# Sums of weight quarters in the delta-net projection, by accumulating DMAs instead of GpSimd arithmetic

## The reference, cut to what matters

```python
def gated_deltanet(h, w_in, conv_w, a_log, dt_bias, norm_w, w_out):   # h: 512 x 1024
    proj = h @ w_in                      # w_in: 1024 x 4112, float32
    qkv, z, a, bt = jnp.split(proj, ...) # q, k, v, z: 8 heads x 128 columns each
    qkv = silu(causal_dwconv(qkv, conv_w))
...
```

## Time and profile before

| What | Value |
|---|---|
| device time, median of 3 runs | 2596.41 us (2595.0 to 2597.74) |
| span of the profiled execution | 2595.1 us |
| PE busy | 2532.1 us (98% of the span) |
| DVE busy | 1643.4 us (63%) |
| POOL busy | 252.9 us (10%), of it 91.4 us in the four lines of sums |
| bytes moved by DMA | 276.81 MB |
| delta-net with its projection | from 40 us to about 450 us of the span |

### The profile page before, as it was taken

How to read it: one execution, slowest core, us unless ns; L and a number is a source line. 1 busy time by engine, 2 the same in 40 slices (tenths; PEclk the granted TensorE clock), 3 DMA queues, 4 the chain that set the end, 5 groups by cost and what they waited for, 6 DMA issues and landing times.

```text
span 2595.1 us, 32921 instructions
## 1 busy us (share of the span) xinstructions
PE 2532.1 (98%) x13038; PEld 1999.9 (77%) x13038; DVE 1643.4 (63%) x2905; ACT 719.3 (28%) x1381; POOL 252.9 (10%) x186
## 2 busy tenths in 40 slices
PE   6999999999999999999999999999999999999999
PEld 3777775688888888888888888886445568888888
DVE  2787875687776365455648777745375486666652
ACT  3555553321110122211203111004253375222200
POOL 1434331100000030000001000001121000000000
PEclk9999999999999999999999999999999999999999
DMA  8222311243433321122023453331021310212121
GB/s 350 109 79 74 131 74 72 91 185 146 188 142 144 120 77 70 69 83 84 33 97 130 163 195 148 137 122 69 33 83 65 130 66 33 93 70 98 67 90 55
DMA packets 26377, 276.81 MB, mean 107 GB/s; under 512 B 3689, under 2 KB 4585, under 8 KB 9201
## 3 DMA queue, kind: packets, MB, share of 16 engines
q1 hardware_dynamic: 23040, 268.92, 27.1%
q10 hardware_dynamic: 3184, 5.78, 0.7%
HBM read 272.58 MB, written 2.11 MB: 106 GB/s over the span
## 4 chain that ended last, share of the span: by engine, by line
PE 87%; DVE 7%; ACT 3%; DMA 2%; issue 1%; POOL 0%; SPq 0%; ACTq 0%; DVEq 0%; POOLq 0%
PE bank L688 29%; PE bank L772 15%; PE bank L2583 11%; PE bank L1467 5%; PE bank L2996 5%; PE bank L2369 4%; PE bank L419 3%; DVE arena L1906 1%; PE bank L2674 1%; DMA arena<-w_ada 1%; PE bank L501 1%; PE bank L2989 1%; PE bank L1617 1%; PE bank L1605 1%; PE bank L3139 1%
## 5 line engine op out<-in xcount | busy, mean ns | idle before, releaser
L688 PE MATMUL bank<-HT,ring 128*128 128x256 f32 x1056 | 248.0, 380 | 2.0 <-ACT HT L1104 2.0
L688 PE MATMUL bank<-arena,ring 128*128 128x256 f32 x1056 | 249.5, 379 | 0.0
L688 PE MATMUL bank<-arena 128*128 128x256 f32 x1056 | 249.5, 379 | 0.0
L688 PEld LDWEIGHTS bank<-HT,ring 128*128 128x128 f32 x1056 | 199.3, 190 | 34.2 <-issue 5.2
L688 PEld LDWEIGHTS bank<-arena,ring 128*128 128x128 f32 x1056 | 200.6, 190 | 27.3
L688 PEld LDWEIGHTS bank<-arena 128*128 128x128 f32 x1056 | 200.6, 190 | 27.3
L772 PE MATMUL bank<-arena,ring 128*128 128x256 f32 x936 | 207.0, 379 | 1.4 <-ACT arena L845 1.4
L772 PEld LDWEIGHTS bank<-arena,ring 128*128 128x128 f32 x936 | 177.4, 190 | 27.1 <-ACT arena L845 2.6
L1328 ACT ACTIVATE arena<-bank,ffc 128x512 f32<-128x512 f32 x66 | 51.3, 777 | 487.3 <-DVE bank L1234 487.3
L1133 POOL TENSOR_SCALAR XT<-XT,comb_v 128x512 f32<-128x512 f32 x32 | 50.1, 1577 | 1049.3 <-ACT HT L1104 652.3
L2996 PE MATMUL bank<-HT,ring 128*128 128x512 f32 x320 | 146.5, 598 | 0.5 <-ACT HT L1145 0.5
(11 more groups left out here) (509 smaller groups left out, 4403.5 us busy)
## 6 DMA issues: line engine op xcount, KB each, us to landing
ring<-w_ada SPq DMA_DIRECT2D x33, 2048.0 KB, 7.5
ring<-w_up SPq DMA_DIRECT2D x33, 2048.0 KB, 7.4
ring<-w_down SPq DMA_DIRECT2D x24, 1408.0 KB, 6.0
ring<-w_gdn SPq DMA_DIRECT2D x7, 2048.0 KB, 8.9
ring<-w_ret_qk SPq DMA_DIRECT2D x4, 2048.0 KB, 8.2
ring<-w_ret_v SPq DMA_DIRECT2D x4, 2048.0 KB, 8.2
ring<-w_ret_g SPq DMA_DIRECT2D x4, 2048.0 KB, 8.3
ring<-w_ret_out SPq DMA_DIRECT2D x4, 2048.0 KB, 8.3
```

Of the source, the lines that this page charges most:

```text
L688: last = nc.tensor.matmul(out_, w[:, k, :], x[:, k, :], start=(first and k == 0), stop=(k == 3), skip_group_check=not first)
```

## The change

The four sums of a pair become DMAs of 256 KB with `accum_op=add`, issued from POOL's queue. A DMA can only add, so S3 = A11 + A21, S2 = S3 + A22, S1 = A21 + A22 and S4 = A12 + S2 are made, and the signs are turned in the input's sums and where the results are put together. S3, S2 and S1 add a quarter that is read again from the weights in memory; S4 adds S2 from SBUF. For S1 the place of A11 must first hold A21: ACT loads it anew from memory (256 KB, plain) behind `keep_m1`, after a wait for S3's landing. PE waits for the landings in place of POOL's counter. POOL waits for S2's landing before it issues S4, and for ACT's load before S1. Ten semaphores are added.

```diff
+        gdn_sum_in = {name: [sem(f"gdn_{name}_in{p}") for p in range(2)] for name in ("S1", "S2", "S3", "S4", "A21")}
...
-                        pe.wait_ge(pool_done, at("pool", "gdn", "S3", h, p))
+                        pe.wait_ge(gdn_sum_in["S3"][p], 16 * (h + 1))
...
                 nc.scalar.activation(gdn_m1, B[p][:, 0:TH], ACT.Copy).then_inc(act_done, AC.tick("gdn", "m1", h, p))
+                act.wait_ge(gdn_sum_in["S3"][p], 16 * (h + 1))
+                A11, u = gdn_quarters(h, p)[0], GDN_UNITS[p][1]
+                act.dma_start(A11.rearrange("p k n -> p (k n)"), dr["w"]["gdn"][h][:, u * KC * P:u * KC * P + 4 * P]).then_inc(gdn_sum_in["A21"][p], 16)
...
-                nc.vector.tensor_tensor(gdn_t, Bg[:, TH:T], gdn_m7, ALU.add).then_inc(dve_done, DV.tick("gdn", "t", h, p))
+                nc.vector.tensor_tensor(gdn_t, gdn_m7, Bg[:, TH:T], ALU.subtract).then_inc(dve_done, DV.tick("gdn", "t", h, p))
...
-            nc.vector.tensor_tensor(gdn_T[2], HR[:, 4:8, :], HR[:, 0:4, :], ALU.subtract).then_inc(dve_done, DV.tick("gdn", "T3"))
+            nc.vector.tensor_tensor(gdn_T[2], HR[:, 0:4, :], HR[:, 4:8, :], ALU.subtract).then_inc(dve_done, DV.tick("gdn", "T3"))
...
+            def quarter_in_memory(h, p, n, side):
+                c = GDN_UNITS[p][n] * KC * P + side * 4 * P
+                return dr["w"]["gdn"][h][:, c:c + 4 * P]
...
-                nc.gpsimd.tensor_tensor(A21, A11, A21, ALU.subtract).then_inc(pool_done, PO.tick("gdn", "S3", h, p))
+                pool.dma_start(flat(A21), quarter_in_memory(h, p, 0, 0), accum_op=ALU.add).then_inc(gdn_sum_in["S3"][p], 16)
...
                 pool.wait_ge(pe_done, at("pe", "gdn", "M7", h, p))
-                pool.wait_ge(pool_done, at("pool", "gdn", "S3", h, p))
-                nc.gpsimd.tensor_tensor(A21, A22, A21, ALU.subtract).then_inc(pool_done, PO.tick("gdn", "S2", h, p))
-                pool.wait_ge(pool_done, at("pool", "gdn", "S2", h, p))
-                pool.wait_ge(pe_done, at("pe", "gdn", "M1", h, p))
-                nc.gpsimd.tensor_tensor(A11, A11, A21, ALU.add).then_inc(pool_done, PO.tick("gdn", "S1", h, p))
+                pool.wait_ge(gdn_sum_in["S3"][p], 16 * (h + 1))
+                pool.dma_start(flat(A21), quarter_in_memory(h, p, 1, 1), accum_op=ALU.add).then_inc(gdn_sum_in["S2"][p], 16)
+                pool.wait_ge(gdn_sum_in["A21"][p], 16 * (h + 1))
+                pool.dma_start(flat(A11), quarter_in_memory(h, p, 1, 1), accum_op=ALU.add).then_inc(gdn_sum_in["S1"][p], 16)
+                pool.wait_ge(gdn_sum_in["S2"][p], 16 * (h + 1))
                 pool.wait_ge(pe_done, at("pe", "gdn", "M2", h, p))
-                nc.gpsimd.tensor_tensor(A12, A12, A21, ALU.subtract).then_inc(pool_done, PO.tick("gdn", "S4", h, p))
+                pool.dma_start(flat(A12), flat(A21), accum_op=ALU.add).then_inc(gdn_sum_in["S4"][p], 16)
```

More of the change, by code:

```diff
@@ L1454, in pe_steps @@
                     if k == 0:
-                        pe.wait_ge(pool_done, at("pool", "gdn", "S1", h, p))
+                        pe.wait_ge(gdn_sum_in["S1"][p], 16 * (h + 1))
                         if p == 0:
@@ L1460, in pe_steps @@
                     if k == 0:
-                        pe.wait_ge(pool_done, at("pool", "gdn", "S2", h, p))
+                        pe.wait_ge(gdn_sum_in["S2"][p], 16 * (h + 1))
                 else:
@@ L1464, in pe_steps @@
                     if k == 0:
-                        pe.wait_ge(pool_done, at("pool", "gdn", "S4", h, p))
+                        pe.wait_ge(gdn_sum_in["S4"][p], 16 * (h + 1))
                         pe.wait_ge(dve_done, at("dve", "gdn", "t", h, p))
@@ L1925, in U2 @@
                 dve.wait_ge(dve_done, DV.n)
-                nc.vector.tensor_tensor(gdn_U2, Bx[:, TH:T], gdn_m1, ALU.add).then_inc(dve_done, DV.tick("gdn", "U2", h, p))
+                nc.vector.tensor_tensor(gdn_U2, Bx[:, TH:T], gdn_m1, ALU.subtract).then_inc(dve_done, DV.tick("gdn", "U2", h, p))
             def c21():
@@ L1943, in c12 @@
                 dst = Bg[:, TH:T] if p else raw_q[:, TH:T]
-                nc.vector.tensor_tensor(dst, Bg[:, TH:T], gdn_U2, ALU.add).then_inc(dve_done, DV.tick("gdn", "c12", h, p))
+                nc.vector.tensor_tensor(dst, Bg[:, TH:T], gdn_U2, ALU.subtract).then_inc(dve_done, DV.tick("gdn", "c12", h, p))
             return t, U2, c21, c22, c12
@@ L1952, in dve_gdn @@
             dve.wait_ge(dve_done, at("dve", "gdn", "input", 6))
-            nc.vector.tensor_tensor(gdn_T[2], HR[:, 4:8, :], HR[:, 0:4, :], ALU.subtract).then_inc(dve_done, DV.tick("gdn", "T3"))
-            nc.vector.tensor_tensor(gdn_T[0], HR[:, 0:4, :], HL[:, 0:4, :], ALU.subtract).then_inc(dve_done, DV.tick())
+            nc.vector.tensor_tensor(gdn_T[2], HR[:, 0:4, :], HR[:, 4:8, :], ALU.subtract).then_inc(dve_done, DV.tick("gdn", "T3"))
+            nc.vector.tensor_tensor(gdn_T[0], HL[:, 0:4, :], HR[:, 0:4, :], ALU.subtract).then_inc(dve_done, DV.tick())
             nc.vector.memset(reset[0:GH, :], 1.0).then_inc(dve_done, DV.tick())
@@ L1961, in dve_gdn @@
             nc.vector.memset(reset[0:GH, 0::P], 0.0).then_inc(dve_done, DV.tick())
-            nc.vector.tensor_tensor(gdn_T[1], HR[:, 4:8, :], gdn_T[0], ALU.subtract).then_inc(dve_done, DV.tick())
+            nc.vector.tensor_tensor(gdn_T[1], HR[:, 4:8, :], gdn_T[0], ALU.add).then_inc(dve_done, DV.tick())
             dve.wait_ge(dve_done, DV.n)
@@ L2202, in pool_gdn, with flat @@
             begin(None, None, "gdn")
+            def flat(quarter):
+                return quarter.rearrange("p k n -> p (k n)")
+            def quarter_in_memory(h, p, n, side):
+                c = GDN_UNITS[p][n] * KC * P + side * 4 * P
+                return dr["w"]["gdn"][h][:, c:c + 4 * P]
             def third(h, p):
```

## The result

The changed kernel takes 2653.65 us (median of 4 runs, 2651.34 to 2658.01) against 2595.7 us (4 runs, 2594.88 to 2597.74): ratio 1.0224, 95% interval 1.021 to 1.0239, so 58 us slower. The prediction was 2604.9 us with a range up to 2630: the sign was right, the size far off, and the time lies outside the range.

The account below looks back on a forecast made before the run. PE, busy 98% of the span, bounds the kernel, so only its waits count: start costs 10.1 + 2.8 + 3.4 = 16.3 us, heads gain 4.2 + 3.6 = 7.8, so 8.5 us slower, 2604.9 us; range 2587 to 2630.

Parts of the forecast that it names:

- 12.9 us "at most": Heads: most that PE could win from DVE's slowing, 1.11 us 7 times in level 5, 0.86 us 6 times in the scan.
- The change does not free DVE: Rival: issuing DMAs on POOL may hold DVE as the sums did; only the start's cost remains, 2612.7 us; chance 0.10.
- The signs: DVE's operations: turned signs cost nothing, since count and shapes stay the same.
- SP's queue: Loads: SP's queue carries nothing new; 80 transfers, 21 MB, come beside 277 MB, and big loads have most of a head to land.
- With the DMA engines full I take 7 us for an accumulating transfer and 6 for ACT's plain one.: Start, full DMA engines: assumed times from issue to landing, between 2.6 and 12.7 us, nearer the middle because of own queues.
- I count 0.6 us, 6 times: 3.6 us: Scan: gain counted of the 0.86 us DVE wait, with A21 landing near 222 and S1 at 226.5.
- It would wait 0.7 us: Level 5: M5's first step would wait 0.7 us for S1, leaving 0.6 of 1.11 us gained, 7 times: 4.2 us.
- The clock … Two count: 3.4 us.: Start: three pauses over 2 us lower PE's clock, 1.7 us each; those before M5(0,0) and M5(1,0) count.
- The start, 16.3 us.: Start: M5(0,0) 10.1 us later, M5(1,0) 2.8 us later, lowered clock 3.4 us; cost 16.3 us.
- The sum.: Whole kernel: start's cost 16.3 us less the heads' gain 7.8 us makes 8.5 us slower, 2604.9 us.
- slow landings: Rival: sums land after 6 us, 9 with DMA engines full; start costs 21.3 us, total +32.6, 2629 us; chance 0.13.
- an L of 7.8 us: High end of a sum's time from issue to landing, idle DMA engines: two plain loads and two POOL operations; about 2655 us.

Follow-up runs that it names:

- pair1_dma: Kernel before the change, with accumulating DMAs only for the sums of pair 1 of heads 1 to 7, the rest POOL arithmetic: 2605.36 us, ratio 1.0036.
- clock_kept: Changed kernel plus unread identity products on PE before its wait for S1, 12 in pair 0, 6 in pair 1, from head 1 on: 2644.77 us, ratio 1.0183.
- hold_gdn: Changed kernel, but SP holds the next w_gdn load until S1 of pair 0 has landed: 2622.58 us, ratio 1.0101.

## Why the prediction was wrong

**Right.** What bounds the kernel and what the sums cost there: the waits for DVE in the heads, 12.9 us "at most", are all gone. The rival "The change does not free DVE" did not come true. The page "SBUF — State Buffer" of the Trainium skill, section "Who interferes with whom", lets DVE with two SBUF inputs contend with a GpSimd instruction that reads SBUF; by that rule an issue, if it reads no SBUF, leaves DVE alone. The trace agrees (0.43 us beside issues, 1.38 us beside arithmetic). The places where PE would wait were right too (M7 and M5 of (0, 0), M5 of (1, 0), M5 in level 5 and in the scan), and so was the landing of S1 once the big loads are through: issued at 263.58, M5 is there at 267.74. The signs cost nothing, as assumed; SP's queue was not tested by itself.

**"With the DMA engines full I take 7 us for an accumulating transfer and 6 for ACT's plain one."** This is the term that failed most. S3(0,0) took 10.9 us and A21 in the scan 9.2. I had taken the middle between 2.6 and 12.7 because these transfers have queues of their own. A queue of one's own did not help. The trace's records of single packets show where A21's time goes in the scan shown: its first packet moves 3.5 us after the issue (1.0 us in level 5, with no load in flight), its last at 262.96, and the last packet of the loads ends at 262.71. In all five such scans of heads 1 to 5 A21's packets end within 0.6 us of the load's. (S3(0,0) landed before its series of loads was through, so this is no general rule.)

The Trainium skill, page "DMA: Bandwidth & Descriptors", section "Queues, rings and completion order", says that each DMA engine takes turns between its queues and changes over only at the end of a packet. On that page a packet is a group of some 9 to 17 descriptors; that the trace's packets are such turns is not shown. If a turn is one of the trace's packets, 2 KB for A21 and 16 KB for the loads, A21 gets 2 of 18 parts of the bytes, and at the 426 GB/s of the earlier trace rows its 256 KB take 5.5 us, by estimate. Seen were 5.1 us from its first packet to its last, so turns would explain this part. They do not explain the 3.5 us before the first packet, and other sizes of packets were not tried: why it starts so late stays open.

**"I count 0.6 us, 6 times: 3.6 us" gained in the scan.** It was 5.0 us lost, 6 times. In the sum's own steps: A21 lands 6.25 us after S2's issue, not 3.3; S1 lands 10.4 after it, not 7.75; M5's first step stands at 7.3 after it; a wait of 3.1 us, and behind it 2.7 us of lowered clock in the three groups of products shown (1.22, 1.12 and 3.78 us for 0.70, 0.68 and 1.99), less the 0.86 won: 5.0. The forecast had almost no wait and no lowered clock there.

**"It would wait 0.7 us" in level 5.** It waited 1.8. S1 followed S2's issue by 0.5 us rather than 1.0, but landed after 6.0 rather than 4.5: S2 and S1 are in flight together, each needs all 16 engines for 1.66 us, and S1, the second, lands later for it (4.0 us at best, 5.4 in the median; S2's median is 4.3). With 1.4 us of lowered clock (rows at 239.34 and 240.29 against 0.68 and 1.03) and 1.1 won, that is +2.1 in this head, one of the two where the clock fell. In the mean of seven, by pair1_dma, it is +1.3, instead of -0.6.

**"The clock … Two count: 3.4 us."** Three pauses were foreseen at the start, and the short ones in the heads taken to be harmless. But the clock fell behind all six waits of the scans (2.9 to 4.9 us) and two of the seven in level 5, where no lowered clock was in the sum. As clock_kept shows, this is 9 us from head 1 on, not the sum of the slowed rows.

**The start, 16.3 us.** 20.0. M7 came 9.5 us late (5.6 foreseen), all of it S3's landing; M5(0,0) 13.7 (10.1), with A21 at 5.4 (6 foreseen) and S1 at 5.2 (4.5); M5(1,0) 3.8 (2.8). M7's lowered clock did stay hidden behind A21, as foreseen; that behind M5 cost 3 us (16 products in 6.75 us), not 1.7.

**The sum.** Start +3.7, level 5 7 × (1.3 + 0.6) = 13.3, scan 6 × (5.0 + 0.6) = 33.6: 50.6 us, against the 48.7 by which the forecast missed. The rival "slow landings" had the mechanism at the start (9 us when full) and came to 2629. In the scan it kept A21's landing near 222, so it lost 0.8 us a head there where 5.0 were lost, and it left out the lowered clock in the heads and the sharing of the engines between S2 and S1. That its bound of 2655 is close to the measured time is luck: it rests on an L of 7.8 us, and S1 landed after 4.0 to 6.0.

## What to carry to other kernels

Handing work from an engine to a DMA replaces a short operation by a latency, here 1.3 us by 4 to 6 us, and by 9 to 11 us beside a big load; it paid here only for results whose reader is farther away than that (S3 and S4 from head 2 on), not for the link just ahead of the bounding engine (S1). If DMAs form a chain, look at what else is in flight at each link, not only at the first: holding a load back from one link can put it onto the next. And where an engine slows a neighbour, try first to move its operation by one wait; that gave 9 us here without any DMA, and the whole rewrite cost 58.

## What was not expected of the hardware

- An accumulating DMA of 256 KB held the 16 engines 1.66 us, a plain one from POOL 0.78 us, and only 128 GB/s flowed at a share of 0.89 when sums alone were in flight. Its issue kept POOL's queue 0.9 to 1.4 us, a plain one's 0.55 us.
- A 256 KB transfer on a queue of its own took 9 to 11 us beside the big loads (A21 plain 9.2, S3(0,0) accumulating 10.9), and 2.7 us (plain, from ACT) when it was alone.
- A PE pause of 1.8 us was followed by a granted clock of 0.50, others of 2.1 us (pair1_dma) and 3.0 us (hold_gdn) by one of 1.00. Filling the pauses with idle products kept the clock from head 1 on, but most of the time stayed lost in the wait.
